# Block inverse of the RWKV recurrence on four quadrants of the array instead of two, and chunk sums issued two chunks by turns

## The chip, the cores and the metric

The kernel runs on one core of a Trainium2 chip. The metric is the device time in microseconds of one execution. The engines named below are PE (TensorE, the 128x128 matrix array, whose weight loads are listed apart as PEld), DVE (VectorE), ACT (ScalarE), POOL (GpSimd) and SP (SyncE, which issues the DMAs). SBUF is the on-chip memory with 128 partitions; PSUM holds the matmul results, in 8 banks of 512 fp32 columns per partition.

## What is computed

The reference is a decoder of two blocks with two layers each, on 256 tokens of width 1024, in fp32. The first block's layers hold three mixers side by side, one of which is the RWKV-7 recurrence that the change is about:

```python
def step(state, inp):
    r_t, w_t, k_t, v_t, kk_t, b_t = inp
    sa = jnp.einsum('bhvk,bhk->bhv', state, kk_t)
    state = (state * w_t[:, :, None, :] - sa[..., None] * b_t[:, :, None, :]
             + v_t[..., None] * k_t[:, :, None, :])
    y = jnp.einsum('bhvk,bhk->bhv', state, r_t)
    return state, y
...
_, y = lax.scan(step, state0, tuple(seq_first(t) for t in (r_h, w_h, k_h, v_h, kk, b_h)))
```

It has 4 heads of 64 channels. Beside it a layer has a dilated attention, a latent attention, an output projection and a feed-forward part; the second block has no recurrence.

## The kernel before, in words

**Streams.** All weights are streamed in chunks of 128 x 2048 fp32 (1 MB) through two raw buffers. ACT rounds each half of a chunk to a high part (`w_hi`, L228), DVE subtracts for the low part (`w_lo`, L234), and PE multiplies three times (high x high, low x high, high x low; L1041 to L1043 and L1046 to L1048 in this stage). Each engine runs a list written out by hand, and all ordering between engines is by semaphore waits in these lists. An engine that waits holds back everything behind it in its list.

**The recurrence in chunks.** `stage_mix1` runs once per layer, twice in all. It cuts the 256 tokens into four chunks of 64 (`CL`). A pair of chunks (`t` = 0, 1) lies in the two halves of the partitions (`jj` = 0, 1: partitions 0 to 63 and 64 to 127), `part(x)` is such a half, and `hb` says in which half the channels of a head lie. `grams_pe` makes the 64x64 products of keys and queries, `grams_mask` masks them into `GM` (`GM[..., 2, :]` is the strictly triangular matrix that has to be inverted), `gram_t_pe` makes its transpose from the other side, `rhs_pe` a right-hand side.

**The block inverse.** `XY[:, t, 0]` holds X, the transpose of the growing inverse Y in `XY[:, t, 1]`, for 4 heads (`x`) and 2 halves (`jj`). `inv_start_y`, `inv_start_x` and `inv_start` make the first blocks of size 2. Then five levels `lv` double the block size: `inv_t_pe` (L837) multiplies gram by X, DVE masks the product into `TI` (`inv_t_sb`, L1172), `inv_xy_pe` multiplies Y by T (L846, left out at the last level) and T by Y (L848), and DVE subtracts both from X and Y in one operation (`inv_step`, L1322). Every one of these matmuls is 64 rows by 64 columns by 64: its inputs lie in partitions `part(jj)`, which picks the row half of the array, and its output in `part(jj)` as well, which picks the column half. So the quadrants (row half 0, column half 0) and (1, 1) are used, and (0, 1) and (1, 0) are not. Other lines use all four: in `gram_t_pe` (L820) the row half is `hb` and the column half `jj`, in `carry_pe` (L867, L874) the other way round. `solve_pe` applies Y to the right-hand sides.

**The chunk sums.** `chunk_pe(j)` adds, for chunk `j`, keys times values (L883) and b times solved (L884) for four heads into one PSUM bank. Its row half is `j % 2`, its column half `hb`, and `hb` is its outer loop, so four matmuls in a row go to one quadrant before four go to the next; it is called for j = 0, 1, 2. `state_pe` and DVE's `state` (L1361) carry the sums on.

**What lies around.** On PE the levels are interleaved with the rest of the last projections (L1041 to L1048), the rotation for the dilated attention (`turn_pe`, L943, of which the second call waits for `projected`, DVE's L1223), its scores (`dil_scores_pe`, L949, which waits for `roped`, DVE's L702) and the latent attention's projections (L977, L984, L990, L996, L1001). Each scores call is followed by `dil_max` on DVE. On DVE the levels are interleaved with `lat_norm` (L1327 to L1331), `evacuate` (L1223), `dil_rope` (L700 to L702) and the splits L234. ACT copies the products of `rhs_pe` (`tokens_sb`, L1150) and then takes the root for the latent norm (`lat_root`, L1165, after a table load).

## Time and profile before

| quantity | value |
|---|---|
| time, median of 3 runs (lowest, highest) | 980.02 us (978.7, 984.21) |
| time of the profiled execution | 980.24 us |
| its span, first to last instruction | 978.5 us |
| PE busy | 944.3 us, 97% |
| weight loads | 895.0 us, 91% |
| DVE busy | 680.1 us, 70% |
| ACT busy | 554.8 us, 57% |
| DMA queue with the weights, share of 16 engines' span | 42.7% |
| mean granted clock of PE | 0.996 |

A profile row names the line of the kernel, the engine, the operation and the tiles written and read. An fp32 matmul of this kernel stands in the trace as two MATMUL records of 64x64x64 each (L837 is called 2 layers x 5 levels x 2 x 4 x 2 = 160 times and has 320 records), so a group of 8 calls has 16 records. Timeline rows give the start in us from the span's start, the time from there to the end of the last merged instruction, and the count; rows of lines that alternate overlap in time. The end of a PE record is modelled, so the pace of PE is read from starts to starts.

### The profile page before, as it was taken

The numbers are of one execution on the slowest core, as the hardware profiler recorded it, in microseconds if no ns is written. First come the engines' busy times: TensorE is split into PE (matmuls) and PEld (weight loads), VectorE is DVE, ScalarE is ACT, GpSimd is POOL, SyncE is SP. The second block draws the span as 40 slices with busy tenths as digits, with TensorE's granted clock in tenths as the row PEclk, the third lists the DMA queues.
The fourth block names the chain that finished last, engine by engine and source line by source line (L and its number), as shares of the span: only waits on it lengthen the run. The fifth ranks groups of instructions, "written<-read, shape, count | busy, mean of one in ns | idle before, by whom it ended". The sixth has DMA issues, their size and how long they took to land.

```text
span 978.5 us, 20304 instructions
## 1 busy us (share of the span) xinstructions
PE 944.3 (97%) x8816; PEld 895.0 (91%) x8816; DVE 680.1 (70%) x963; ACT 554.8 (57%) x845; POOL 7.7 (1%) x12
## 2 busy tenths in 40 slices
PE   5899999999999999999999999999999999999996
PEld 5898789999999988888999999998889899989896
DVE  5897567766664579867676666447689677598574
ACT  6773456545443478335654444437387766486565
POOL 0000000000000001000000000000000000000000
PEclk9999999999999999999999999999999999999999
DMA  7452016565554534211356645545344234444231
GB/s 266 164 194 83 2 44 215 181 243 207 184 205 173 175 130 157 102 44 46 129 191 237 247 174 184 205 173 172 131 143 159 86 130 174 171 159 143 93 136 75
DMA packets 22280, 149.87 MB, mean 153 GB/s; under 512 B 2480, under 2 KB 2736, under 8 KB 4912
## 3 DMA queue, kind: packets, MB, share of 16 engines
q1 hardware_dynamic: 22192, 148.58, 42.7%
q8 instruction: 69, 1.13, 0.5%
q14 instruction: 19, 0.16, 0.0%
HBM read 147.26 MB, written 1.05 MB: 152 GB/s over the span
## 4 chain that ended last, share of the span: by engine, by line
PE 72%; DVE 15%; ACT 9%; issue 2%; DMA 1%; DVEq 0%; SPq 0%; ACTq 0%
PE bank L1778 8%; PE bank L1780 8%; PE bank L1779 8%; DVE w_lo L234 6%; ACT w_hi L228 4%; PE bank L1801 3%; PE bank L1800 3%; PE bank L1802 3%; PE bank L1998 3%; PE bank L2000 3%; PE bank L1999 3%; PE bank L1041 2%; ACT act_hi L330 1%; PE bank L1042 1%; PE bank L1043 1%
## 5 line engine op out<-in xcount | busy, mean ns | idle before, releaser
L234 DVE TENSOR_TENSOR w_lo<-w_raw,w_hi 128x1024 fp32r<-128x1024 f32 x264 | 315.7, 1223 | 111.2 <-ACT w_hi L228 110.2
L228 ACT ACTIVATE w_hi<-w_raw 128x1024 fp32r<-128x1024 f32 x264 | 267.3, 1052 | 211.7 <-PE bank L1780 109.6
L1778 PE MATMUL bank<-act_hi,w_hi 128*128 128x256 f32 x704 | 196.8, 280 | 1.6 <-DVE w_lo L234 1.0
L1779 PE MATMUL bank<-act_lo,w_hi 128*128 128x256 f32 x704 | 196.1, 279 | 0.0
L1780 PE MATMUL bank<-act_hi,w_lo 128*128 128x256 f32 x704 | 196.1, 279 | 0.0
L1778 PEld LDWEIGHTS bank<-act_hi,w_hi 128*128 128x128 f32 x704 | 132.2, 188 | 2.4 <-issue 1.4
L1779 PEld LDWEIGHTS bank<-act_lo,w_hi 128*128 128x128 f32 x704 | 133.5, 190 | 0.1
L1780 PEld LDWEIGHTS bank<-act_hi,w_lo 128*128 128x128 f32 x704 | 132.3, 188 | 0.0
L1998 PE MATMUL bank<-act_hi,w_hi 128*128 128x256 f32 x352 | 100.4, 285 | 4.9 <-DVE act_lo L336 2.6
L1801 PE MATMUL bank<-gated_lo,w_hi 128*128 128x256 f32 x352 | 98.5, 280 | 0.0
L1802 PE MATMUL bank<-gated_hi,w_lo 128*128 128x256 f32 x352 | 98.3, 279 | 0.0
L1800 PE MATMUL bank<-gated_hi,w_hi 128*128 128x256 f32 x352 | 98.3, 279 | 0.0
L1999 PE MATMUL bank<-act_lo,w_hi 128*128 128x256 f32 x352 | 97.4, 277 | 0.0
L2000 PE MATMUL bank<-act_hi,w_lo 128*128 128x256 f32 x352 | 97.4, 277 | 0.0
L1041 PE MATMUL bank<-act_hi,w_hi 128*128 128x256 f32 x256 | 77.1, 301 | 14.1 <-DVE w_lo L234 13.8
L1998 PEld LDWEIGHTS bank<-act_hi,w_hi 128*128 128x128 f32 x352 | 66.1, 188 | 8.0 <-DVE w_lo L234 3.4
L1042 PE MATMUL bank<-act_lo,w_hi 128*128 128x256 f32 x256 | 73.1, 286 | 0.0
L1043 PE MATMUL bank<-act_hi,w_lo 128*128 128x256 f32 x256 | 72.9, 285 | 0.0
L1999 PEld LDWEIGHTS bank<-act_lo,w_hi 128*128 128x128 f32 x352 | 66.2, 188 | 0.1
L2000 PEld LDWEIGHTS bank<-act_hi,w_lo 128*128 128x128 f32 x352 | 66.2, 188 | 0.0
L1800 PEld LDWEIGHTS bank<-gated_hi,w_hi 128*128 128x128 f32 x352 | 66.2, 188 | 0.0
L1801 PEld LDWEIGHTS bank<-gated_lo,w_hi 128*128 128x128 f32 x352 | 66.1, 188 | 0.0
(355 smaller groups left out, 1992.4 us busy)
## 6 DMA issues: line engine op xcount, KB each, us to landing
w_raw<-in_w_ffn SPq DMA_DIRECT2D x66, 1024.0 KB, 4.8
w_raw<-in_w_mix SPq DMA_DIRECT2D x65, 1024.0 KB, 4.9
small_w<-in_small SPq DMA_DIRECT2D x2, 1280.0 KB, 8.4
x_res<-in_x_channels SPq DMA_DIRECT2D x4, 256.0 KB, 5.8
w_raw<-in_w_mix SPq DMA_DIRECT2D x2, 512.0 KB, 6.2
mem<-in_mem_channels SPq DMA_DIRECT2D x1, 1024.0 KB, 8.3
gates<-in_mem SPq DMA_DIRECT2D x1, 1024.0 KB, 6.8
out_x<-sb_lom SPq DMA_DIRECT2D x4, 256.0 KB, 2.5
```

Source lines behind the costliest of these rows:

```text
L228: self.nc.scalar.activation(hi, self.piece(self.raw[g % self.RAW], p), ACT.Copy).then_inc(self.hi_ready, 1)
L234: self.nc.vector.tensor_tensor(lo, self.piece(self.raw[g % self.RAW], p), hi.bitcast(fp32), ALU.subtract).then_inc(self.lo_ready, 1)
L1041: TE.matmul(o, hi[:, w], HI[:, k, :], start=(k == 0 and x == 0), stop=False)
L1778: TE.matmul(o, hi[:, w], HI[:, k, :], start=(k == 0 and x == 0), stop=False)
L1779: TE.matmul(o, hi[:, w], LO[:, k, :], start=False, stop=False)
L1780: last = TE.matmul(o, lo[:, w], HI[:, k, :], start=False, stop=(k == KT - 1 and x == 1))
L1800: TE.matmul(out, hi[:, w], GHI[:, k, :], start=(k == 0 and o % 2 == 0), stop=False)
L1801: TE.matmul(out, hi[:, w], GLO[:, k, :], start=False, stop=False)
L1802: last = TE.matmul(out, lo[:, w], GHI[:, k, :], start=False, stop=(k == FK - 1 and o % 2 == 1))
L1998: TE.matmul(o, hi[:, w], h[:, k, :], start=(k == 0 and x == 0), stop=False)
L1999: TE.matmul(o, hi[:, w], l[:, k, :], start=False, stop=False)
L2000: last = TE.matmul(o, lo[:, w], h[:, k, :], start=False, stop=(k == KT - 1 and x == 1))
```

## The change

All eight PSUM banks become one tensor, so that an access pattern can run over the border of two banks. For heads 0 and 2 of each group the X matrices move to the other half of the partitions (`side`), and the matrices are kept in the order 0, 2, 1, 3 (`place`), so that within one bank pair the first two places are in the lower bank and all others in the upper one (`across`). The left factor of the first product is then needed in the other half as well: 8 new matmuls per layer (`gram_swapped_pe`) make it, and one ACT copy of 128x256 (`gram_swapped_sb`) brings it to SBUF. In `inv_t_pe` heads 0 and 2 now read one row half and write the other column half. In `inv_xy_pe` the Y by T product of heads 0 and 2 does so too, and the issue order is written out anew; the T by Y product stays where it was for all heads. `inv_start_y` takes two operations instead of one. `chunk_pe` takes a list of chunks and is called for (0, 1) and then (2,), with the column half and the chunk as inner loops. Nothing else in the lists moves.

```diff
-        self.banks = [ctx.enter_context(nc.psum_tensor(f"bank{i}", [P, 512], fp32)) for i in range(8)]
+        self.PS = ctx.enter_context(nc.psum_tensor("bank", [P, 8 * 512], fp32))
+        self.banks = [self.PS[:, 512 * i:512 * (i + 1)] for i in range(8)]
...
+    GF = K.sb("grams_swapped", [P, 2, 2, CL], c=c)
...
+    side = lambda x, jj: part((x + 1 + jj) % 2)
+    place = lambda x: 2 * (x % 2) + x // 2
+    across = lambda t, places: chunks(K.PS[:, 1024 * t + 384:1024 * t + 384 + 512])[:, places, :]
...
-                        last = TE.matmul(banks[hb][part(jj), at_:at_ + CL], AD[part(hb), i, tok],
+                        last = TE.matmul(banks[hb][side(i, jj), at_:at_ + CL], AD[part(hb), i, tok],
...
+    def gram_swapped_pe(pe):
+        for t in range(NT):
+            for hb in range(2):
+                for jj in range(2):
+                    tok = slice((2 * t + jj) * CL, (2 * t + jj + 1) * CL)
+                    last = TE.matmul(across(1, slice(2 * hb + t, 2 * hb + t + 1))[side(0, jj), 0, :], BD[part(hb), 0, tok],
+                                     AD[part(hb), 0, tok], start=True, stop=True)
+        last.then_inc(*up("gram_swapped"))
...
     def inv_t_pe(pe, lv, t):
         pe.wait_ge(*at("inv_xy", 2 * lv + t + 1))
+        if lv == 0:
+            pe.wait_ge(*at("gram_swapped_sb", 1))
+        out = across(t, slice(0, 4))
         for x in range(4):
             for jj in range(2):
-                last = TE.matmul(banks[t][part(jj), x * CL:(x + 1) * CL], GM[part(jj), 4 * t + x, 2, :],
-                                 XY[part(jj), t, 0, x, :], start=True, stop=True)
+                gram = GM[part(jj), 4 * t + x, 2, :] if x % 2 else GF[side(0, jj), x // 2, t, :]
+                last = TE.matmul(out[part(jj), place(x), :], gram, XY[side(x, jj), t, 0, place(x), :],
+                                 start=True, stop=True)
...
+        def x_part(x, jj):
+            return TE.matmul(out[side(x, jj), place(x), :], XY[part(jj), t, 1, place(x), :],
+                             TI[part(jj), 4 * t + place(x), :], start=True, stop=True)
+
+        def y_part(x, jj):
+            return TE.matmul(out[part(jj), 4 + place(x), :], TI[part(jj), 4 * t + place(x), :],
+                             XY[part(jj), t, 1, place(x), :], start=True, stop=True)
+
+        for x in (0, 2):
+            if lv < 4:
+                x_part(x + 1, 0)
+                x_part(x, 0)
+                x_part(x + 1, 1)
+                y_part(x, 0)
+                x_part(x, 1)
+            else:
+                y_part(x, 0)
+            y_part(x, 1)
+            y_part(x + 1, 0)
+            last = y_part(x + 1, 1)
...
-    def chunk_pe(pe, j):
-        for hb in range(2):
-            for i in range(2):
-                u, jj = unit(j // 2, 2 * i + hb), j % 2
-                o = banks[jj][part(hb), (j // 2 * 2 + i) * CL:(j // 2 * 2 + i + 1) * CL]
-                TE.matmul(o, KTT[part(jj), u, :], VT[part(jj), u, :], start=(i == 0), stop=False)
-                last = TE.matmul(o, BTT[part(jj), u, :], WU[part(jj), u, 1, :], start=False,
-                                 stop=(j == 0 and i == 1))
-        last.then_inc(*up("chunk_sum"))
+    def chunk_pe(pe, js):
+        for i in range(2):
+            for n in range(2):
+                for hb in range(2):
+                    for j in js:
...
+    def gram_swapped_sb(act):
+        act.wait_ge(*at("gram_swapped", 1))
+        S.activation(GF.rearrange("p b t c -> p (b t) c"), across(1, slice(0, 4)), ACT.Copy).then_inc(*up("gram_swapped_sb"))
...
-        ch.post(V.tensor_tensor(XY[:, t, 1, :, :], GM[:, 4 * t:4 * t + 4, 2, :], each(cst("nlev0"), 4), ALU.mult))
+        for i in range(2):
+            ch.post(V.tensor_tensor(XY[:, t, 1, 2 * i:2 * i + 2, :], GM[:, 4 * t + i:4 * t + 4:2, 2, :],
+                                    each(cst("nlev0"), 2), ALU.mult))
...
-        V.tensor_tensor(xy, xy, chunks(banks[2 + t][:, first * T:2 * T]),
+        V.tensor_tensor(xy, xy, across(t, slice(4 * first, 8)),
```

The order of PE around the right-hand side, in layer 0, before (L820 is `gram_t_pe`, L829 `rhs_pe`):

```order
L820 MATMUL bank<-rwkv_bufs 64x64 [waits grams_sb]
L820 MATMUL bank<-rwkv_bufs 64x64 x15
L829 MATMUL bank<-rwkv_bufs,grams 64x64 [waits tokens,grams_sb]
L829 MATMUL bank<-rwkv_bufs,grams 64x64 x15
L1041 MATMUL bank<-act_hi,w_hi 128x256 [waits lo_ready]
```

and in the changed kernel, where L826 is `gram_t_pe`, L844 `rhs_pe` and L835 the new `gram_swapped_pe`:

```order
L826 MATMUL bank<-rwkv_bufs 64x64 [waits grams_sb]
L826 MATMUL bank<-rwkv_bufs 64x64 x15
L844 MATMUL bank<-rwkv_bufs,grams 64x64 [waits tokens,grams_sb]
L844 MATMUL bank<-rwkv_bufs,grams 64x64 x15
L835 MATMUL bank<-rwkv_bufs 64x64 x8
L1076 MATMUL bank<-act_hi,w_hi 128x256 [waits lo_ready]
```

The 8 new matmuls stand behind the right-hand side and ahead of the next projection. The order of ACT at the same place in the changed kernel, where L1185 is `tokens_sb`, L1207 `gram_swapped_sb` and L1200 `lat_root`:

```order
L1185 ACTIVATE rwkv_bufs<-bank 128x8x64 [waits tokens_T] x2
L1207 ACTIVATE grams_swapped<-bank 128x256 [waits gram_swapped]
L1200 ACT_TABLE_LOAD
L1200 ACTIVATE rope_a<-bank,prm 128x256 [waits lat_ss]
```

The copy stands between the copies for the right-hand side and the table load. The order of PE within the first product group of level 0, `inv_xy_pe(0, 0)`, before (L846 makes Y by T, L848 T by Y):

```order
L846 MATMUL bank<-inv_t,inv_xy 64x64 [waits inv_t]
L848 MATMUL bank<-inv_xy,inv_t 64x64
L846 MATMUL bank<-inv_t,inv_xy 64x64
L848 MATMUL bank<-inv_xy,inv_t 64x64
L846 MATMUL bank<-inv_t,inv_xy 64x64
```

and in the changed kernel, whole (L865 makes Y by T, L869 T by Y):

```order
L865 MATMUL bank<-inv_t,inv_xy 64x64 [waits inv_t]
L865 MATMUL bank<-inv_t,inv_xy 64x64 x2
L869 MATMUL bank<-inv_xy,inv_t 64x64
L865 MATMUL bank<-inv_t,inv_xy 64x64
L869 MATMUL bank<-inv_xy,inv_t 64x64 x3
L865 MATMUL bank<-inv_t,inv_xy 64x64 x3
L869 MATMUL bank<-inv_xy,inv_t 64x64
L865 MATMUL bank<-inv_t,inv_xy 64x64
L869 MATMUL bank<-inv_xy,inv_t 64x64 x3
```

The number of matmuls, 16, is the same; what goes to which quadrant and in which turn is new.

## Rows read from the trace of the kernel before

**Rows 1.** The page: busy time, and PE's granted clock in 40 slices.
```profile
PE 944.3 (97%) x8816; PEld 895.0 (91%) x8816; DVE 680.1 (70%) x963; ACT 554.8 (57%) x845; POOL 7.7 (1%) x12
PEclk9999999999999999999999999999999999999999
```
**Rows 2.** Stretches: from:to and length, then busy time (instructions) of PE, PEld, DVE, ACT, POOL.
```profile
76.00:90.20 14.20, 14.18 (x267) 12.13 (x266) 12.20 (x21) 2.21 (x3) 0.00 (x0) 1.00 0.01 2
90.20:116.00 25.80, 25.80 (x366) 19.61 (x366) 16.59 (x37) 11.00 (x28) 0.00 (x0) 1.00 0.12 43
```
**Rows 3.** PE's timeline, layer 0, level 0, two quadrants: start, us, line, count.
```profile
76.02 1.15 PE L837 MATMUL bank<-inv_xy,grams 64*64 64x64 f32 x32
77.09 0.39 PE L1041 MATMUL bank<-act_hi,w_hi 128*128 128x256 f32 x1
...
78.67 0.34 PE L846 MATMUL bank<-inv_t,inv_xy 64*64 64x64 f32 x4
...
79.19 0.33 PE L846 MATMUL bank<-inv_t,inv_xy 64*64 64x64 f32 x4
...
79.42 0.33 PE L846 MATMUL bank<-inv_t,inv_xy 64*64 64x64 f32 x4
...
80.73 1.98 PE L943 MATMUL bank<-proj,consts_both 128*128 128x512 f32 x4
```
**Rows 4.** PE's timeline, layer 0: groups that use all four quadrants, and what follows.
```profile
69.97 0.69 PE L820 MATMUL bank<-rwkv_bufs 64*64 64x64 f32 x32
70.62 1.15 PE L829 MATMUL bank<-rwkv_bufs,grams 64*64 64x64 f32 x32
...
114.10 0.46 PE L867 MATMUL bank<-rwkv_bufs,solved 64*64 64x64 f32 x16
114.38 0.68 PE L874 MATMUL bank<-grams,solved 64*64 64x64 f32 x24
114.99 1.12 PE L996 MATMUL bank<-small_w,probsT 128*128 128x512 f32 x2
```
**Rows 5.** PE's timeline, layer 0: the chunk sums' first row and what follows them.
```profile
116.05 0.33 PE L883 MATMUL bank<-rwkv_bufs 64*64 64x64 f32 x2
...
118.09 1.53 PE L525 MATMUL bank<-consts_both,probs 128*128 128x128 f32 x12
```
**Rows 6.** DVE's timeline, layer 0, before level 0.
```profile
68.95 0.42 DVE L1303 TENSOR_TENSOR inv_xy<-grams,consts_first 128x256 f32<-128x256 f32 x1
69.28 1.28 DVE L1297 TENSOR_TENSOR grams<-bank,consts_first 128x512 f32<-128x512 f32 x2
...
71.95 0.88 DVE L1308 TENSOR_TENSOR inv_xy<-bank,consts_first 128x128 f32<-128x128 f32 x4
```
**Rows 7.** DVE's timeline, layer 0, levels 0 and 1.
```profile
76.75 0.89 DVE L1172 TENSOR_TENSOR inv_t<-bank,consts_first 128x256 f32<-128x256 f32 x2 [1.80 <-PE bank L837]
...
80.59 1.28 DVE L1322 TENSOR_TENSOR inv_xy<-inv_xy,bank 128x512 f32<-128x512 f32 x2
...
84.02 0.76 DVE L1172 TENSOR_TENSOR inv_t<-bank,consts_first 128x256 f32<-128x256 f32 x2
...
86.56 0.69 DVE L1322 TENSOR_TENSOR inv_xy<-inv_xy,bank 128x512 f32<-128x512 f32 x1 [0.66 <-PE bank L848]
87.50 0.69 DVE L1322 TENSOR_TENSOR inv_xy<-inv_xy,bank 128x512 f32<-128x512 f32 x1 [0.25 <-PE bank L848]
...
89.42 0.69 DVE L702 TENSOR_TENSOR small_w<-rope_a,rope_b 128x512 f32<-128x512 f32 x1
```
**Rows 8.** PE's timeline, layer 0: the scores, and layer 1's right-hand side with its wait.
```profile
90.17 0.71 PE L949 MATMUL bank<-small_w 64*128 64x128 f32 x8
...
398.12 1.15 PE L829 MATMUL bank<-rwkv_bufs,grams 64*64 64x64 f32 x32 [0.28 <-DVE grams L1297]
```
**Rows 9.** ACT's timeline, layer 0, around the root of the latent norm.
```profile
72.43 1.28 ACT L1165 ACT_TABLE_LOAD   x1
74.60 0.47 ACT L1165 ACTIVATE rope_a<-bank,prm 128x256 f32<-128x256 f32 x1 [0.89 <-PE bank L967]
```

More of the change, by code:

```diff
@@ L1456, in _ @@
         rhs_pe(pe)
+        gram_swapped_pe(pe)
         proj(pe, 7, (2,))
@@ L1499, in _ @@
         lat_value_pe(pe, 1)
-        for j in range(3):
-            chunk_pe(pe, j)
+        chunk_pe(pe, (0, 1))
+        chunk_pe(pe, (2,))
         dil_turn_pe(pe)
```

20 lines of the change are left out of this document (10 added, 10 removed).

## The prediction, made before the changed kernel ran

> **What bounds the kernel now.** I read the page first. PE is busy for 944.3 us, 97% of the span, and its clock is at its upper level (2.4 GHz) in all 40 slices [rows 1]. The table of stretches says the same of the part that the change touches: between 76.0 and 90.2 us, and from there to 116.0, PE leaves next to no time idle, and DVE is busy for 12.20 of 14.20 us in the first stretch but only for 16.59 of 25.80 in the second [rows 2]. So what PE saves can shorten the kernel, but in the first stretch DVE is close behind it. The layer's start and the rest of the kernel follow PE and keep their length, so I need the shift of one recurrence stage, and take it twice (layer 1 runs the same list 327.5 us later: L829 at 70.62 and at 398.12 [rows 4, 8]).
>
> **The pace of a quadrant.** In the inverse, rows of four records each come 0.23 us apart (79.19 and 79.42) while the other line's rows run in between, so 8 records take 0.234 us, over two quadrants: one record each 29 ns, and one per 58.5 ns in each quadrant [rows 3]. A group of 32 records over two quadrants thus takes 16 x 0.0585 = 0.94 us, and 0.13 more until the next full-array matmul starts (76.02 to 77.09 is 1.07) [rows 3]. Over four quadrants, 32 records take at most 0.65 us from start to start, and 16 take 0.28 [rows 4]. And where four quadrants are loaded unevenly (L874: 24 records, 8 of them in each of the two fullest), the group takes 0.61 = 8 x 0.0585 + 0.14 [rows 4]. So the fullest quadrant sets the length. This is what the whole sum is built on.
>
> The Trainium skill, page "TensorE: Matmul & The Clock Gate", section "The mechanism" of its part on packing small matmuls, says that a weight load overlaps with running matmuls only when its row group differs. By that rule two quadrants of one row half would take turns, four quadrants would be no faster than two, and the sum would have no gain in it at all. L820's 0.65 us for 32 records [rows 4] speaks against it: taking turns would need 0.94.
>
> **The change, part by part, for one layer.**
>
> 1. First product (`inv_t_pe`): a group of 16 records had 8 in each of two quadrants and gets 4 in each of four. Saves 4 x 0.0585 = 0.234 us; 10 groups, 2.34 us.
>
> 2. Second product (`inv_xy_pe`), levels 0 to 3: of 8 matmuls for two heads, quadrants (0, 0) and (1, 1) had 4 each; now they have 3 each and the other two one each. A group of 32 records goes from 16 to 12 records deep, 0.94 to 0.70 us: again 0.234 saved, 8 groups, 1.87 us. The bounds: nothing, if the uneven turns stall the queue, and 0.47 per group if four quadrants were filled evenly, which they are not. I take 0.234, by L874, the uneven row. Level 4 has only products that stay where they were: nothing.
>
> 3. Chunk sums: 48 records took from 116.05 to 118.09, 2.04 us [rows 5], although the two column halves were both in use, since 8 records in a row go to one quadrant. Now (0, 1) is 32 records over four quadrants, 8 deep, and (2,) 16 records over two, 8 deep: 16 x 0.0585 + 0.14 = 1.08. Saves 0.96 us.
>
> 4. The swapped gram: 16 new records over four quadrants cost PE 0.28 us, by the 16 records of L867 [rows 4]. Its ACT copy (0.47 us, as the root's own 128x256 operation) lands ahead of the table load at 72.43; the root behind that load waited 0.89 us for PE [rows 9]. PE needs the copy at 76.0 [rows 3]. It costs nothing beyond PE's 0.28.
>
> 5. `inv_start_y` in two operations: a 128x256 operation takes 0.33 us to the next start (68.95 to 69.28), two of 128x128 take 0.44 (four in 0.88) [rows 6]: 0.1 us more. The mask behind it ends at 70.56 (69.28 + 1.28) [rows 6], and PE's right-hand side starts at 70.62 in layer 0 [rows 4] and waits 0.28 us for that mask in layer 1 [rows 8]. So PE is late by 0.1 us. The second such operation has the 1.80 us of idle DVE before level 0 to hide in [rows 7].
>
> PE alone: 2.34 + 1.87 + 0.96 - 0.28 - 0.10 = 4.8 us saved per layer.
>
> **What of it reaches the end.** I follow DVE through levels 0 and 1, in shifts against before. PE starts level 0 later by 0.10 + 0.28 = 0.38; its first product is ready 0.234 sooner, so DVE, which waited for it [rows 7], starts its chain at +0.15. That chain (mask of T, latent norm, evacuation, step 0, rope 0, mask of T at 84.02, split, to 85.90, which is 86.56 less the 0.66 of idle) is nearly closed: of the stretch's 2.0 idle us [rows 2], 0.75 lie before 76.75, 0.66 and 0.25 before the two steps [rows 7], which leaves 0.3 for all else. So it stays at +0.15. PE meanwhile is 0.55 early at `turn_pe`, whose second matmul, half of 1.98 us behind the first [rows 3], is the one that needs the evacuation: at 80.73 - 0.55 + 0.96 = 81.1, and the evacuation lies ahead of the step at 80.6 [rows 7], so it is over by 80.8. No wait. But level 1's second product needs DVE's mask: 84.02 + 0.42 + 0.15 + 0.06 = 84.65, where PE, which was there at 86.56 - 0.94 - 0.26 = 85.36 and is now 0.55 + 0.47 early, would be at 84.3. A new wait of 0.3 us. The split ends at 86.05, then come the two steps, which used to wait 0.66 and 0.25 us for PE [rows 7]: the first at 86.05, the second 0.60 later at 86.65 (its product is there at 84.65 + 2 x 0.70 + 0.26 = 86.3, with 0.26 from 76.02 + 0.47 to 76.75). It stood at 87.50, so the shift is -0.85. Rope 1 follows at once and ended at 89.42 + 0.69 = 90.11 before [rows 7], and the scores of the dilated attention start at 90.17 [rows 8]: they already waited for DVE. They now start at -0.85, though PE alone would have them at about -1.5. So levels 0, 1 and the first product of level 2, which save PE 2.34, less 0.38, bring 0.85 and not 1.96.
>
> Behind the scores DVE is idle for 9 of 25.8 us [rows 2], so I put no further wait there; that is the least certain step, and the range's upper end covers it. The four remaining group pairs (second product of level 2, both of level 3, first of level 4) bring 4 x 0.47 = 1.87, the chunk sums 0.96. One layer: 0.85 + 1.87 + 0.96 = 3.7 us; two layers 7.4. Against the profiled execution of 980.24 us that is 972.8; the median of the runs is 0.2 us lower, 972.6.
>
> **Rivals.**
>
> A. The uneven second product gains nothing, because its turns (three in quadrant (0, 0), one in (0, 1)) stall PE's queue. For: the chunk sums of before, with 8 records in a row to one quadrant, took 2.04 us and not 24 x 0.0585 = 1.40 + 0.14, so the queue looks ahead only so far [rows 5]. Against: the new order never puts more than four records of one quadrant in a row, which is what the inverse has now at full pace [rows 3]. Lost: 0.47 at each of levels 2 and 3, and about 0.17 in DVE's chain at level 1: 1.1 per layer. 975.0 us.
>
> B. DVE is no bound at level 1 (its operations are shorter there by enough, or PE's products come early enough), and all 4.8 us of PE count: 970.6 us.
>
> C. Slower, by DVE: its operands now run over the border of two banks, which no row of before shows. Eight such operations (two masks and two steps in each of levels 0 and 1) lie in the chain that ends in the scores. The gain of a layer is gone when each takes 0.46 us longer (3.7 / 8). If each took its own time once more (0.42 and 0.64 [rows 7]), the chain would be 4.2 us longer: 3.4 late instead of 0.85 early at the scores, less 2.8 behind them, 0.6 us lost per layer, 981.4 us. Against: the operation streams as many elements as before.
>
> D. Not what it says: quadrants of one row half take turns. Then each group lasts as long as before (4 of 8 matmuls in each row half), the swapped gram costs 8 x 0.0585 + 0.05 = 0.5 and the mask 0.1: 981.4 us, slower. L820 is against it, for equal loads of the quadrants.
>
> **How the numbers follow.** Forecast 0.67, A 0.13, B 0.10, C 0.06, D 0.04. Layer shifts from -2.6 (A) to -4.8 (B) give 970.6 to 975.0; the runs of before scatter by 4.2 us above the median and 1.3 below, so I widen to 969.5 and 976.5, which leaves C, D and some scatter outside. About 0.5% (4.9 us) is what a measurement of this kernel can tell from no change. Faster by more than that means below 975.1: the forecast, B, and half of A, less a little for scatter, 0.81. C and D lie mostly within 0.5%: same 0.16, slower 0.03.
>
> **What would show it.** The first products: 16 records in about 0.37 us to a full-array matmul, not 0.6. The two second-product groups of a level: from 2.06 [rows 3] to about 1.6 us. Chunk sums to the transposes: 1.1 us. PE's scores: idle time before them, put down to DVE's rope, of some 0.6 us, and a wait for the mask at level 1. DVE's masks and steps: still 0.42 and 0.69 us. Any longer, and C is at work; a second product at 2.06 would be A or D, with the first product telling which. I would be wrong if DVE's chain started late for another reason, or if the saved time came back as waits in the attention part behind the chunk sums, where the trace of before has PE and DVE in step.

## The result, and the profile of the changed kernel

The changed kernel ran in 969.85 us (median of 4 executions, 965.98 to 969.95) against 979.75 us before (978.7 to 984.21). The ratio is 0.9889 [0.9861, 0.9918]. A second comparison, with more executions (changed 970.71 us, 965.62 to 975.33, six executions; before 979.32 us, 29 executions), gave 0.9921 [0.9893, 0.995]. So it is faster by 0.8 to 1.1%, which is 7.7 to 10.9 us of the median of before, and the forecast was 7.4. The profiled execution took 965.98 us with a span of 964.2, against 980.24 and 978.5 before. That difference of 14.3 us is more than the change gives, and the parts of it are told below.

The page of the changed kernel, the rows that answer to [rows 1] (busy time, share of the span, instructions; then the granted clock in 40 slices):

```profile
PE 930.4 (96%) x8848; PEld 881.2 (91%) x8848; DVE 679.2 (70%) x967; ACT 555.0 (58%) x847; POOL 7.7 (1%) x12
PEclk9999999999999999999999999999999999999999
```

The two stretches that answer to [rows 2], from level 0 to the scores and from the scores to the chunk sums:

```profile
75.60:88.30 12.70, 11.96 (x266) 9.74 (x266) 11.81 (x21) 2.35 (x3) 0.00 (x0) 1.00 0.02 5
88.30:112.20 23.90, 23.90 (x366) 17.74 (x366) 16.46 (x37) 10.89 (x28) 0.00 (x0) 1.00 0.14 46
```

The first is 1.5 us shorter and PE has 0.74 us idle in it, where it had none. The second is 1.9 us shorter with no idle time on PE, the 1.87 us forecast for its four group pairs. In the first DVE is busy for 11.81 of 12.70 us.

PE's timeline of the changed kernel in layer 0 answers to [rows 3], [rows 4], [rows 5] and [rows 8] (L826 was L820, L856 was L837, L865 was L846, L920 was L883, L526 was L525):

```profile
69.33 0.69 PE L826 MATMUL bank<-rwkv_bufs 64*64 64x64 f32 x32
...
75.75 0.27 PE L856 MATMUL bank<-inv_xy,grams_swapped 64*64 64x64 f32 x2
75.77 0.27 PE L856 MATMUL bank<-inv_xy,grams 64*64 64x64 f32 x2
...
76.38 0.39 PE L1076 MATMUL bank<-act_hi,w_hi 128*128 128x256 f32 x1
...
77.96 0.35 PE L865 MATMUL bank<-inv_t,inv_xy 64*64 64x64 f32 x8
...
79.51 1.98 PE L978 MATMUL bank<-proj,consts_both 128*128 128x512 f32 x4
...
88.30 0.71 PE L984 MATMUL bank<-small_w 64*128 64x128 f32 x8 [0.74 <-DVE small_w L708]
...
112.27 0.34 PE L920 MATMUL bank<-rwkv_bufs 64*64 64x64 f32 x8
...
113.35 0.88 PE L526 MATMUL bank<-consts_both,probs 128*128 128x128 f32 x6
```

The reader should take three sums from it. The first products of a level (32 records) last from 75.75 to 76.38, 0.63 us, and lasted 1.07. The second products last from 77.96 to 79.51, 1.55 us, and lasted 2.06. The chunk sums last from 112.27 to 113.35, 1.08 us, and lasted 2.04. All three are what the prediction computed from the fullest quadrant (0.60, 1.6 and 1.1). PE waits for DVE's rope at the scores, as forecast.

I follow the gain through layer 0 as the start in the changed kernel less the start before, at the same instruction:

| place in layer 0 | before | after | shift | since 69.97 |
|---|---|---|---|---|
| gram_t | 69.97 | 69.33 | -0.64 | 0 |
| first product of level 0 | 76.02 | 75.75 | -0.27 | +0.37 |
| after the first products of level 0 | 77.09 | 76.38 | -0.71 | -0.07 |
| rotation (turn) | 80.73 | 79.51 | -1.22 | -0.58 |
| scores | 90.17 | 88.30 | -1.87 | -1.23 |
| transposes behind the chunk sums | 118.09 | 113.35 | -4.74 | -4.10 |

The first 0.64 us were there before the first changed instruction of PE. They come from the start of the kernel: at this place two kernels with the same code up to it stand 1.3 us apart (69.97 in before, 68.71 in chunk_only of experiment 2). Layer 1 goes from -4.75 to -8.89, -4.14 in all. Together the recurrence gives 8.2 us in this pair of profiles, not 7.4. The remaining 5.4 us of the 14.3 lie behind it and are no work of the change's own instructions: 4.4 us come up to the wait near 828 us, from a pace of PE that differs between executions (experiment 1), 1.2 us from that wait (experiment 5), and 0.3 us are lost again between it and the end.

### The profile page after: what moved, and what is told of

The parts are those of the page before. It is cut to its first block, busy times and chain, and to the rows that moved or that the text cites. A ratio compares the mean times of both kernels' runs of the same rounds, so it can differ in the third digit from the quotient of the medians.

```text
span 964.2 us, 20378 instructions
## 1 busy us (share of the span) xinstructions
PE 930.4 (96%) x8848; PEld 881.2 (91%) x8848; DVE 679.2 (70%) x967; ACT 555.0 (58%) x847; POOL 7.7 (1%) x12
## 4 chain that ended last, share of the span: by engine, by line
PE 69%; DVE 19%; ACT 9%; issue 3%; DMA 0%; DVEq 0%; SPq 0%; ACTq 0%
PE bank L1821 8%; PE bank L1822 8%; PE bank L1823 8%; DVE w_lo L234 6%; PE bank L2041 4%; PE bank L1844 4%; PE bank L1843 4%; PE bank L1845 3%; ACT w_hi L228 3%; PE bank L2043 3%; PE bank L2042 3%; PE bank L2046 2%; ACT act_hi L331 2%; PE bank L2048 2%; PE bank L2047 2%
```

## The experiments

### 1. Both kernels once more: which part of 14 us belongs to the kernel?

r_before and r_after are the two kernels as they are.

> The kernel before, once more, to see how its runs scatter and to have a second trace of it. The traces so far show that the full-array matmuls of the projections run at one of two paces, one start every 113 or every 118 ns, for whole stages at a time (118 in the second layer's feed-forward part before, 113 in the profiled execution after). Theory T (the change moves only the two recurrence stages, 4.1 us each; the pace of the other stages varies from execution to execution): ratio 1.000 within 0.004, and the stages' paces in this trace differ somewhere from the first trace of before. Rival R (the pace is a property of the kernel): the same paces in the same stages as in the first trace, 118 ns in the second feed-forward part.

> The changed kernel, once more. T: a median of 969.5 to 971.5 us, ratio 0.990, with single runs some 4 us apart where a stage changes its pace; the two recurrence stages again 4.1 us shorter each. R: the second feed-forward part at 113 ns again.

Measured: r_before 979.29 us (974.81 to 984.61, 12 executions), ratio 1.0007 [0.9981, 1.0032]; r_after as told above. The profiled execution of r_before took 975.75 us, 4.5 less than the 980.24 of the same kernel's first profile. The tables of stretches show where. This is the first line of the gate and up matmuls of the feed-forward stage, before (L1778), in layer 0 and in layer 1:

```profile
200.00:260.00 60.00, 48.67 (x178) 33.17 (x177) 1.00 0.60 219
520.00:580.00 60.00, 47.75 (x170) 31.84 (x171) 1.00 0.61 227
```

And the same stretches of r_before:

```profile
200.00:260.00 60.00, 48.72 (x177) 33.14 (x177) 1.00 0.60 216
520.00:580.00 60.00, 48.70 (x178) 33.21 (x177) 1.00 0.62 228
```

The code is identical and the granted clock is 1.00 in all four, yet PE starts 177 or 178 matmuls of that line in 60 us in three of them and 170 in one. With the two lines beside it that is one start every 112 or 118 ns. Taken over 24 starts each, the medians are 113 or 118 ns, and from the fourth chunk of a stage on one of the two holds for all its gate and up matmuls. One stage at the slower pace costs 4.5 us. So the 82 executions of before that were measured beside the experiments stand in three heaps: 32 near 975.4, 38 near 979.7 and 12 near 984 us. The profiled executions of all kernels but pauses fit this: none, one or two slow feed-forward stages in the trace go with the lowest, the middle or the highest heap of the kernel. The changed kernel's ten have heaps near 965.8 (two), 970 (six) and 974.8 (two). Compared heap by heap, by their means, the change is worth 9.2 to 9.6 us. A median of three or four executions can lie in any heap, which is enough to make the two ratios differ.

The recurrence stages keep their length from r_before to before within 0.03 us. Those of r_after do not do what was expected: layer 0 is 4.16 us shorter than in before, layer 1 only 3.52. PE stands still there inside the right-hand side's group, for a reason that experiment 6 comes to.

What follows: the profiled pair (before with one slow stage, after with none) overstates the change by 4.5 us.

### 2. Each half of the change alone

chunk_only puts the new chunk sums into the kernel before. inverse_only is the changed kernel with the old chunk sums; this is its call, beside which `chunk_pe` has its old body again:

```diff
-        chunk_pe(pe, (0, 1))
-        chunk_pe(pe, (2,))
+        for j in range(3):
+            chunk_pe(pe, j)
```

> The kernel before with the new chunk sums alone (two chunks by turns). By the trace of after, chunk sums take 0.96 us less per layer and nothing waits behind them: 1.9 us in all, 977.9 us, ratio 0.998. If the queue of PE did not matter, 0 us.

> The changed kernel with the old chunk sums. T: 1.9 us longer than the changed kernel, about 971.8 us, ratio 0.992; its recurrence stages are 3.15 us shorter each than before. If the gains of the two parts were not additive (one hides the other), it would equal the changed kernel.

Measured: chunk_only 981.75 us (977.35 to 983.06, 12 executions), ratio 1.0024 [1.0009, 1.004]. inverse_only 974.48 us (968.45 to 977.17), ratio 0.9956 [0.9933, 0.9979]. By its time alone chunk_only is slower than before, where 977.9 was expected. Its trace says otherwise. PE's timeline of chunk_only in layer 0, first and last rows:

```profile
115.13 0.34 PE L886 MATMUL bank<-rwkv_bufs 64*64 64x64 f32 x8
...
116.22 1.53 PE L525 MATMUL bank<-consts_both,probs 128*128 128x128 f32 x12
```

The chunk sums take 1.09 us instead of 2.04. Over them the shift against before goes from -0.92 to -1.87 in layer 0 and from +1.88 to +0.93 in layer 1: 0.95 us each, the forecast's 0.96. The loss is elsewhere: both feed-forward stages of the profiled execution ran at 118 ns, and ten of its 12 executions lie near 982, in the heap of two slow stages, where 12 of the 82 of before lie. Heap by heap chunk_only is 2.0 us faster than before (982.0 against 983.9, and its other two at 977.6 against 979.7), and 1.9 had been expected. If each execution drew its pace by itself at the odds of before, ten or more of 12 in the slowest heap would come less than once in a million times. So this kernel meets the slow pace more often, at least where it was measured; why is open. The new chunk sums alone are not enough for it: the changed kernel has them too, and two of its ten executions are in its slowest heap.

inverse_only was expected near 971.8 us and came out at 974.48, again by the mixture: one execution lies in its lowest heap, five near 972.9 and six near 976.7, which is 6.8 to 7.3 us below the heaps of before. Its profile has both stages at 113 ns. From the projection behind the right-hand side to the transposes its layers are 3.51 and 3.50 us shorter than in before, those of the changed kernel 4.43 and 4.46, so the chunk sums make 0.9 to 1.0 us of the difference. The whole of its layer 1 gains only 2.26 us, since it has the same standstill as r_after.

What follows: the two halves add up on the path and heap by heap (2.0 and 6.8 to 7.3 of 9.2 to 9.6 us); the medians do not show it.

### 3. Does one PSUM tensor matter by itself?

```diff
-        self.banks = [ctx.enter_context(nc.psum_tensor(f"bank{i}", [P, 512], fp32)) for i in range(8)]
+        self.PS = ctx.enter_context(nc.psum_tensor("bank", [P, 8 * 512], fp32))
+        self.banks = [self.PS[:, 512 * i:512 * (i + 1)] for i in range(8)]
```

> The kernel before with the eight banks as slices of one PSUM tensor, and nothing else: no instruction changes. T: ratio 1.000. Rival R2 (the single tensor changes addresses or paces and so carries the 1.7 to 2.5 us that the forecast missed): 977.5 us, ratio 0.9975.

Measured: 979.29 us (975.81 to 984.1, 12 executions), ratio 1.0 [0.9979, 1.0021]. No effect is seen, to 0.2%. DVE's operations on operands over the bank border, which only the changed kernel has, take no longer either. DVE's timeline of the changed kernel, layer 0, answers to [rows 7]:

```profile
76.28 0.76 DVE L1211 TENSOR_TENSOR inv_t<-bank,consts_first 128x256 f32<-128x256 f32 x2 [1.80 <-PE bank L856]
...
79.99 1.27 DVE L1363 TENSOR_TENSOR inv_xy<-inv_xy,bank 128x512 f32<-128x512 f32 x2
...
83.23 0.76 DVE L1211 TENSOR_TENSOR inv_t<-bank,consts_first 128x256 f32<-128x256 f32 x2
...
85.04 1.28 DVE L1363 TENSOR_TENSOR inv_xy<-inv_xy,bank 128x512 f32<-128x512 f32 x2
...
87.55 0.69 DVE L708 TENSOR_TENSOR small_w<-rope_a,rope_b 128x512 f32<-128x512 f32 x1
```

Two masks take 0.76 us (0.76 at level 1 before, and 0.89 with a short wait between them at level 0) and two steps 1.27 or 1.28, as before. Rival C (8 such operations, each 0.46 us longer) is out.

### 4. The order of the second product, and how far the queue looks ahead

plain_order writes the second product head by head and half by half; grouped sends the matmuls of a quadrant one behind the other, so that six in a row go to (0, 0) and six to (1, 1), twelve records each. The work in each quadrant is the same in all three orders:

```diff
 plain_order
+        for x in range(4):
+            for jj in range(2):
+                if lv < 4:
+                    x_part(x, jj)
+                last = y_part(x, jj)
...
 grouped
+        for jj in range(2 if lv < 4 else 0):
+            x_part(0, jj)
+            x_part(2, jj)
+        for jj in range(2 if lv < 4 else 0):
+            x_part(1, jj)
+            x_part(3, jj)
+            for x in range(4):
+                last = y_part(x, jj)
```

> The changed kernel with the second product in the plain order of heads and halves, Y by T and T by Y in turns as before, instead of the written-out order. Up to four records of one quadrant stand in a row, as in the kernel before. Theory Q: same as the changed kernel, 969.9 us, groups of 0.70 us. Rival A of the prediction (uneven turns stall): groups of 0.8 to 0.94 us, 971 to 974 us.

> The changed kernel with the second product's 16 matmuls issued by quadrant (2 and 2 to the two light quadrants, then 6 in a row to (0, 0), then 6 in a row to (1, 1)). Same matmuls, same load of each quadrant. Theory Q (PE's queue looks only some four records ahead, which is why the old chunk sums took 2.04 us): a group takes 20 turns of 58.5 ns, 1.17 us, instead of 12, 0.70; with the waits on DVE that it causes, some 3.5 us per layer, 977 us. Rival (only the sum per quadrant counts, order does not): 969.9 us.

Measured: plain_order 969.98 us (966.62 to 974.16, 6 executions), ratio 0.9917 [0.9892, 0.9942]; grouped 973.21 us (971.9 to 977.08, 7 executions), ratio 0.9947 [0.9923, 0.9972]. The profile of grouped has both feed-forward stages at 113 ns and took 971.9 us; that of the changed kernel, also with both at 113, took 965.98. Two rows of PE's timeline of grouped show the cost at level 0:

```profile
77.31 0.47 PE L865 MATMUL bank<-inv_t,inv_xy 64*64 64x64 f32 x12
...
79.76 1.98 PE L977 MATMUL bank<-proj,consts_both 128*128 128x512 f32 x4
```

The two groups take 2.45 us instead of 1.55, 0.9 us more; four levels in two layers have them, 7.2 us at most. The recurrence stages are 0.82 and 0.84 us shorter than in before, where the changed kernel's are 4.10 and 4.14, so 6.6 us of them reach the end; heap by heap it is 6.6 to 6.9. Expected were 3.5 us per layer. The medians (973.21 against some 970) show only half of it, since five of the seven executions of grouped lie in its lowest heap. The length of a group is the 1.17 us of the expectation (2 x 1.17 + 0.13 = 2.47). The fullest quadrant has the same 12 records per group, so the rule "the fullest quadrant sets the length" needs a second half: the order has to offer another quadrant soon enough. Orders with two (the written-out one) and four records in a row (plain_order) run at full pace. Twelve in a row do not, and neither do eight: the old chunk sums took 2.04 us for what now takes 1.08. What lies between four and eight was not tried.

plain_order gains what the written-out order gains (its recurrence of layer 0 takes 4.08 us less, against 4.10; its layer 1 takes 3.18 less, with the standstill of r_after in it), so the elaborate order brings nothing over the plain one, and rival A (uneven turns gain nothing) is out.

The Trainium skill, page "TensorE: Matmul & The Clock Gate", section "The mechanism", was the ground of rival D: a weight load overlaps only with another row group. In all three orders two quadrants of one row half worked at once (32 records in 0.63 us at the first product, where turns within a row half would need 16 x 0.0585 = 0.94). So the turns that the prediction drew from the rule do not happen with these 64x64 matmuls. Whether a weight load overlaps a running matmul of its own row half these rows can't show, since the end of a PE record is modelled.

### 5. The wait near 828 us

In the second block, far behind the change, PE of the kernel before waits once for 1.29 us, because ACT's split waits for a weight chunk. Rows of PE's and of ACT's timeline, before:

```profile
828.59 0.39 PE L1998 MATMUL bank<-act_hi,w_hi 128*128 128x256 f32 x1 [1.29 <-DVE act_lo L336]
```

```profile
818.70 1.06 ACT L228 ACTIVATE w_hi<-w_raw 128x1024 fp32r<-128x1024 f32 x1 [1.21 <-DMA w_raw<-in_w_mix]
```

The same ACT row of the changed kernel has no wait:

```profile
804.17 1.06 ACT L228 ACTIVATE w_hi<-w_raw 128x1024 fp32r<-128x1024 f32 x1
```

The DMA view of the stretch in which this chunk is on its way, before (queue: packets, MB, share; then median us to landing):

```profile
q8 instruction: 1, 0.02, 1.6%
...
w_raw<-in_w_mix SPq DMA_DIRECT2D x2, 1024.0 KB, 6.0
```

And of the changed kernel, where that view has no line of the instruction queue:

```profile
w_raw<-in_w_mix SPq DMA_DIRECT2D x2, 1024.0 KB, 4.8
```

The instruction queue q8 moves pieces of 16 KB, 70 in the changed kernel, for 17,913 instructions of PE in its trace: about 256 each, and they start in step with PE's progress, so it most likely carries PE's program. In all four profiles with the old inverse and nothing added (before, r_before, chunk_only, merged_psum) a piece starts 0.9 to 1.1 us behind the issue of this chunk, which then lands after 5.7 to 6.0 us, and PE waits 1.04 to 1.43 us. In all eight with the new inverse no piece does, the chunk lands after 4.8 to 5.2 us, and PE's wait is 0.2 us or less in five; 0.40, 0.46 and 0.36 us of it are left in inverse_only, plain_order and best. The traces of these eight have 68 instructions of PE more than that of before. Two kernels test this. code_pad adds nothing but instructions, before PE's first matmul, where PE waits anyway:

```diff
+        if layer == 0:
+            for _ in range(68):
+                pe.wait_ge(sem("prm_in"), 16)
         proj(pe, 0)
```

swap_alone (on merged_psum) adds the swapped gram of the change and its ACT copy, unused:

```diff
         rhs_pe(pe)
+        gram_swapped_pe(pe)
...
+        gram_swapped_sb(act)
         lat_root(act)
```

> The kernel before with 68 waits on an event long past, on PE ahead of its first matmul, where PE waits some 4 us for the first split anyway. No work changes; PE's program is 68 instructions longer, as in the changed kernel. Theory 'code position': every 16 KB transfer of the instruction queue comes about 68 instructions earlier against the work, none falls beside the weight chunk that is issued near 812.7 us, that chunk lands in about 4.8 us instead of 6.0, PE's wait of 1.3 us near 828 us is gone, and the runs are 1.2 us faster than the kernel before (clusters near 973.9 and 978.4 instead of 975.1 and 979.6). Rival 'timing': nothing moves, 979.5 in the median and the wait is there.

> The kernel before (with its PSUM as one tensor) plus the swapped gram alone: 8 matmuls and one ACT copy per layer, whose result nobody uses; level 0 waits for the copy as in the changed kernel. It measures the added work of the change by itself. The prediction's price: 0.28 us of PE per layer and nothing for ACT, so level 0 starts 0.28 us later in each layer, +0.56 us by the end of the recurrence stages. It also lengthens PE's program by 64 instructions and the waits, and so tests the wait of 1.3 us at the start of the second block's second layer. Theory 'code position' (a 16 KB transfer of the instruction queue falls beside the landing of one weight chunk in every kernel with the old program length, 5.7 to 6.0 us to landing instead of 4.8, and beside none with the new length): the wait is gone here too, and the median is 0.6 us below the kernel before. Rival 'timing' (the wait goes because the recurrence ends several us sooner): the wait stays, and the median is 0.6 us above.

Measured: code_pad 977.32 us (975.31 to 979.67, 12 executions), ratio 0.9994 [0.9968, 1.0019]; swap_alone 979.04 us (975.08 to 982.92, 12 executions), ratio 1.0007 [0.9983, 1.0032]. 1.2 us can't be seen in these times: the executions of code_pad lie near 976 and 979, those of before near 975.4 and 979.7, and not 1.2 us lower. In the traces it can. ACT's rows, first of code_pad, then of swap_alone:

```profile
817.35 1.06 ACT L228 ACTIVATE w_hi<-w_raw 128x1024 fp32r<-128x1024 f32 x1 [0.66 <-DMA w_raw<-in_w_mix]
```

```profile
817.65 1.06 ACT L228 ACTIVATE w_hi<-w_raw 128x1024 fp32r<-128x1024 f32 x1
```

In swap_alone ACT's wait is gone and PE's is down to 0.12 us, although its recurrence is not shorter but longer: the shift against r_before goes from +4.75 ahead of the place to +3.59 behind it. That rules out that the wait went because the recurrence ended sooner. In code_pad the piece starts with the issue of the chunk (811.89) and not 1.1 us behind it, the chunk lands after 5.4 us, and ACT waits 0.66 instead of 1.21 us, PE 0.77 instead of 1.29. A full disappearance had been expected. The trace has a reason for the half: the 68 waits stand in it as 34 instructions (17,879 against 17,845 before), where the changed kernel and swap_alone have 68 more. Counted by the instructions that PE had yet to run, the piece comes 18 to 20 of them earlier than in before and r_before; in the changed kernel and in swap_alone it comes some 50 earlier.

That a piece slows the transfer beside it does not rest on this place alone. In the 14 profiles, behind 70 us, 1708 weight chunks were issued. Of 78 that had a piece start 1 to 3 us behind their issue, 65 took more than 5.6 us to land; of 1087 with no piece beside them, 20 did, with a median of 4.8 us. A piece that starts 4 us or more behind the issue costs next to nothing (4.9 us in the median), and those are the most (374), so that the median over all chunks with a piece moves by 0.1 us only. A piece isn't the only cause either: the next chunk of plain_order landed after 6.0 us without one.

swap_alone also prices the added work: PE comes to the next projection 0.24 us later in layer 0, against 0.28 forecast. In layer 1 it comes 0.94 us later, because PE stands still there inside the right-hand side's group (0.49 us put down to "issue"), as in r_after; the changed kernel, which has no such standstill in its first profile, has 0.24 us in both layers. The ACT copy costs nothing: the root behind it still waits 0.85 us for PE (it waited 0.89, [rows 9]).

```profile
71.78 0.38 ACT L1180 ACTIVATE grams_swapped<-bank 128x256 f32<-128x256 f32 x1
72.18 1.28 ACT L1184 ACT_TABLE_LOAD   x1
74.31 0.47 ACT L1184 ACTIVATE rope_a<-bank,prm 128x256 f32<-128x256 f32 x1 [0.85 <-PE bank L982]
```

### 6. Taking back what DVE holds

The 0.74 us at the scores and the mask ahead of the right-hand side are the two places in the recurrence stage where the changed kernel waits for DVE. scores_later moves the scores behind the next quarter of projection 8:

```diff
-        dil_scores_pe(pe, 0)
         proj(pe, 8, (3,))
+        dil_scores_pe(pe, 0)
```

> The changed kernel with the dilated attention's first scores behind the last quarter of the projection instead of ahead of it. In the trace of after PE waits 0.74 us there for DVE's rotation. T: the wait goes, nothing takes its place (DVE needs the scores only 1.1 us after their end), 0.7 us per layer, 1.4 in all: 968.5 us. Rival: the wait comes back at the second product of level 2, or at the latent queries, which wait for the maxima of these scores: no gain.

Measured: 968.68 us (965.82 to 969.0, 6 executions), ratio 0.989 [0.987, 0.9911]. From the projection behind the right-hand side to the transposes the layers gain 4.92 and 4.90 us, and 4.43 and 4.46 in the changed kernel: 0.9 us in all come on top, where 1.4 had been expected. The times don't show it, since the intervals overlap and the lowest execution (965.82) is no lower than the changed kernel's (965.62). Part of the 0.74 returns one step later, 0.38 us in layer 0 and 0.3 in layer 1 (the expectation of best puts it at 0.57):

```profile
91.48 1.97 PE L1012 MATMUL bank<-probsT,small_w 128*128 128x256 f32 x8 [0.38 <-DVE neg_max L495]
```

best puts the scores in the middle of that quarter, and `inv_start_y` behind the mask that PE waits for:

```diff
-        inv_start_y(dve, ch, 0)
         grams_mask(dve, 1)
         st.split_lo(dve, 8, 1)
+        inv_start_y(dve, ch, 0)
         inv_start_y(dve, ch, 1)
...
+        proj_part(pe, 8, 3, (6,))
         dil_scores_pe(pe, 0)
-        proj(pe, 8, (3,))
+        proj_part(pe, 8, 3, (7,))
```

> The changed kernel with two moves. (a) `inv_start_y` for the first pair of chunks stands behind `grams_mask(dve, 1)` and the split on DVE, instead of ahead of it: the changed kernel splits that operation in two and PE waits about 0.35 us at `rhs_pe` for the mask behind it. (b) the first scores of the dilated attention stand in the middle of the last quarter of projection 8 (six matmuls before, six behind); with them behind the whole quarter (scores_later) 0.57 us of wait came back at the latent queries. Theory 'PE is the bound and each of these waits lies on its path': (a) takes 0.3 us off each layer, (b) 0.4 more than scores_later, so the recurrence stages end 1.4 us earlier than in scores_later, median about 967.3 us. Rival 'DVE's chain carries it on': DVE ends level 1 no earlier, because the same operations are only in another order, so (a) comes back as a longer wait before the scores or the queries, and the median is that of scores_later, 968.7.

Measured: 967.68 us (964.56 to 974.65, 6 executions), ratio 0.9907 [0.9869, 0.9944]. Its lowest execution is 1.1 us below the lowest of the changed kernel. That it beats scores_later is not shown, the intervals overlap. That its median is near the expected 967.3 is luck, for the trace does not have the expected parts. Both waits are gone in layer 0:

```profile
87.97 0.72 PE L984 MATMUL bank<-small_w 64*128 64x128 f32 x8
...
91.27 1.97 PE L1012 MATMUL bank<-probsT,small_w 128*128 128x256 f32 x8
```

But from the projection behind the right-hand side to the transposes its layers gain 4.91 and 4.89 us, the same as scores_later: move (b), from which 0.4 us were expected, brought nothing more. Move (a) brings PE from `gram_t_pe` to the right-hand side 0.23 and 0.43 us sooner than in the changed kernel, and 0.3 had been expected.

In layer 1 a gap of 1.12 us stands inside the right-hand side's group, and the profile finds nothing that PE waits for:

```profile
396.63 0.92 PE L844 MATMUL bank<-rwkv_bufs,grams 64*64 64x64 f32 x24
398.67 0.27 PE L844 MATMUL bank<-rwkv_bufs,grams 64*64 64x64 f32 x2 [1.12 <-issue]
```

It is no fault of this kernel's moves. The second profile of the changed kernel, which has the same code as the first, has it at the same place, and the first has not:

```profile
397.65 0.91 PE L844 MATMUL bank<-rwkv_bufs,grams 64*64 64x64 f32 x24 [0.35 <-DVE grams L1336]
398.99 0.27 PE L844 MATMUL bank<-rwkv_bufs,grams 64*64 64x64 f32 x2 [0.43 <-issue]
```

Of the nine profiles whose traces have 17,913 instructions of PE, six have it: r_after 0.43 us, swap_alone 0.49, inverse_only 0.72, plain_order 0.73, pauses 0.72 and best 1.12. In best a piece of PE's program starts at 396.3, and the one before it started at 375.1. In all six the late piece comes 20.8 to 21.3 us behind the one before it, PE stops at the same instruction (some 530 behind the start of the earlier piece, two pieces and more), and it goes on 2.3 to 2.4 us after the late piece has started. In the other three (after, grouped, scores_later) the piece comes 16.1 to 17.3 us behind the one before it, and there is no gap. In the shorter program of before the interval was 20.2 us without a gap. So PE most likely ran out of instructions. Why the piece is sometimes late wasn't tried. The right-hand side's group of layer 1 is longer by 0.6 to 1.3 us for it, which takes back part of what the change gives in these executions.

### 7. When is the pace of experiment 1 set?

pauses is the changed kernel in which PE also waits for the next chunk's split, ahead of four chunks of each feed-forward stage:

```diff
+        if p == 0 and i in (6, 10, 14, 18):
+            st.arrived(pe, i + 1, 0)
```

> The changed kernel with four pauses of PE in each feed-forward stage: ahead of chunks 6, 10, 14 and 18 it also waits for the split of the next chunk, 2 to 3 us each, 16 to 24 us in all. The gate and up matmuls (128x256 each) have run at one start every 113 ns or one every 118 ns, one pace for all chunks of a stage. Theory 'the pace is set anew when PE has been idle': the stretches between pauses of one stage differ, some at 113 and some at 118 ns, in at least one of the two layers. Rival 'the pace belongs to the stage or to the execution': all stretches of a layer have one pace. If all ten stretches show the same pace, it tells neither apart, except that a fair draw would do that seldom.

Measured: 1001.51 and 998.93 us. The four pauses of layer 0 are in PE's waits (us in total, times, longest):

```profile
PE bank L1823 <- issue: 10.8, 4, 2.7
```

Within layer 0 all starts between 157 us and the first pause at 187.8 are 118 ns apart, and 113 in the four stretches behind it, once PE is back at full clock. Within layer 1 it is 118 ns from 510 us up to the last pause at 607.3 and 113 behind it. Three rows of the table of stretches, for one of the three lines, with the clock as the third number from the end. At the full clock it starts 60 times in 20 us at the faster pace and 58 times at the slower; the first row has part of its time at a lower clock:

```profile
220.00:240.00 20.00, 15.92 (x57) 10.98 (x57) 0.95 0.41 154
245.00:265.00 20.00, 16.22 (x60) 11.01 (x60) 1.00 0.47 163
532.00:552.00 20.00, 15.88 (x58) 10.66 (x57) 1.00 0.47 167
```

So the pace is no property of the stage or of the execution: it can change where PE has stood still. In the kernels without pauses it can change at the odd matmuls behind the third chunk (`spread`), and from there it holds for 90 us. It did not change at every pause, and what decides it is open. The pauses differ in one more thing: behind five of the eight PE first started every 203 to 213 ns, with a granted clock of 0.79 over the 8 us around the pause, and behind three it kept the clock at 1.00. Both changes of pace came behind a pause with the lower clock, none of those three brought one. So this run can't tell whether standing still or the clock's fall and rise sets the pace anew; behind `spread`, where it changed too, the clock stayed at 1.00. Pauses are no cure: this kernel takes 1000 us.

## Why the prediction was wrong, step by step

The forecast was 972.6 us in a range of 969.5 to 976.5. The first comparison's ratio puts the changed kernel at 0.9889 x 980.02 = 969.1, below the range, though its plain median of 969.85 is just inside; the second ratio puts it at 972.3, near the forecast. On which side of the bound it falls is luck, for the step from heap to heap is over 4 us. By heaps the change is worth some 9.4 us and not 7.4. The direction and the mechanism were right and the size was short by 2 us: 0.8 in the recurrence (DVE's chain, below) and 1.2 behind it (the wait near 828 us).

**The pace of a quadrant: right.** All four quadrants work at once at one record per 58.5 ns each. First products, second products and chunk sums came out at 0.63, 1.55 and 1.08 us against 0.60, 1.6 and 1.08. What the step lacked is experiment 4's condition on the order. It was in the text only as an argument against rival A, and that argument (never more than four records of one quadrant in a row) held.

**The added work: right as far as it was priced.** The swapped gram 0.24 us (0.28 forecast), its ACT copy nothing. The mask later by 0.10: right, PE's wait for it in layer 1 went from 0.28 to 0.38 us. What the working put at nothing is what 68 more instructions do to the arrival of PE's program: in six of nine profiles the right-hand side's group of layer 1 is 0.6 to 1.3 us longer for it, so "take it twice" does not hold in those executions.

**DVE through levels 0 and 1: the step that failed.** The prediction had 2.0 us of idle time on DVE, gave 1.66 to known places, and went on: "which leaves 0.3 for all else. So it stays at +0.15." That remainder was, it seems, waiting for PE, at the second mask of level 0 and ahead of the first rope operation, for both gaps are gone in the changed kernel; they are too short for the view to name what ended them. The pair of masks at level 0 fell from 0.89 to 0.76 us, and the mask of level 1 starts at 83.23 instead of 84.02: 0.79 sooner, of which 0.64 are the earlier start of the stage, so the chain stood at -0.15 and not at +0.15. With 0.3 us less on DVE the new wait of PE at level 1's second product, which was forecast, did not appear, and the scores came at -1.23 instead of -0.85. That is 0.4 us in each layer: 4.10 and 4.14 instead of 3.7.

**The wait at the scores: right in kind.** It was forecast as some 0.6 us and was 0.74, and experiment 6 shows that it held back 0.4 to 0.5 us per layer. Behind the scores no wait came back: from there to the transposes 2.87 us were gained, and the forecast was 2.83.

**"The rest of the kernel follow PE and keep their length": wrong by 1.2 us.** The wait near 828 us went with the length of PE's program. Nothing in the working put a price on what the number of instructions does to the queue that carries them.

**The scatter: misread.** The range took the runs of before (978.7 to 984.21) as noise around one value. They are heaps some 4.3 us apart, and the three runs shown had none from the lowest heap, where 32 of 82 lie. A median of four executions can be a heap away from another, and the profiled pair was.

**The rivals.** Their four times start from the profiled execution (980.24) and the forecast's from the median, so they are 0.2 us high, which changes nothing. A is out by experiment 4, C by experiment 3, and D by the first products, which take 0.63 us and not 1.07. B (all 4.8 us of PE count) is out as it was put, since PE does wait for DVE at the scores, but it was nearer in size: 4.1 lies between 3.7 and 4.8, and with the scores moved the layer gives 0.4 to 0.5 us more.

## What to carry to other kernels

Small matmuls of 64 rows and columns run on four quadrants at once and cost what the fullest quadrant holds, provided that the program does not send too many records in a row to one of them: up to four were free here, eight and twelve were not. An engine's idle time that is left over in a sum can be a wait for the engine that the change makes faster, as it was here: look it up, instruction by instruction, before you call a chain closed. And when a kernel's runs stand in heaps, compare heap with heap, or the same stretch of two traces, before you believe a difference of one heap.

## What the runs showed of the chip that was not expected

- Full-array matmuls of 128x256 have two paces at the full granted clock, one start per 113 ns or per 118 ns. The gate and up matmuls of a stage keep one of them for about 90 us, which makes 4.5 us; it differs between executions of one kernel and can change where PE has been idle. One kernel (chunk_only) met the slow one far more often than before did. What chooses it is open.
- PE's program arrives, most likely, in pieces of 16 KB (256 instructions). Of the 1 MB weight chunks that had a piece start 1 to 3 us behind their issue 65 of 78 took more than 5.6 us to land, of those without a piece 20 of 1087. So 68 more instructions in one place took a wait of 1.2 us away in another, 700 us later.
- PE can stand still for want of a piece: 0.43 to 1.12 us in six of nine profiles with the longer program, always at the same instruction and always when the piece came 20.8 us or more behind the one before it.
- Records in a row to one quadrant cost nothing up to four; twelve cost 0.9 us per level (2.45 against 1.55 us), eight 0.96 us per layer in the chunk sums.
- DVE reads an operand that runs over the border of two PSUM banks in the time of one within a bank (0.76 us for two of 128x256, 1.27 for two of 128x512).
